# Second modulation part of the first two mixers: multiplied and added up on GpSimd between its transfers, one sum over the rows on TensorE

## Chip, cores and metric

One core of one Trainium2 chip. The metric is the device time of one execution in microseconds, median of several runs.

## What is computed

Four transformer layers on 256 tokens of width 1024, in fp32. Layers 0 and 1 have a mixer of attention, short convolution and spatial gating, and behind it a PEER layer that gathers expert rows; layers 2 and 3 have a gated linear attention and a recurrent mixer, and a mixture of 16 experts. Every layer is steered by six vectors that come from one conditioning vector, and these are what the change is about:

```python
mod = (c_act @ w_ada + b_ada)[:, None, :]            # c_act [1, 1024], w_ada [1024, 6144]
sh1, sc1, g1, sh2, sc2, g2 = jnp.split(mod, 6, axis=-1)
h = rms_norm(x, norm1_g) * (1 + sc1) + sh1
...
x = x + g1 * (merged @ w_out)
h2 = rms_norm(x, norm2_g) * (1 + sc2) + sh2
x = x + g2 * peer_ffn(h2, ...)
```

## The kernel before

**Modulation pieces.** A layer's `w_ada` is cut into three parts of 2048 columns (part 0: sh1, sc1; part 1: g1, sh2; part 2: sc2, g2), and each part into eight pieces of 128 rows x 2048 columns, 1 MB each. Piece number i is 24 x layer + 8 x part + k. The eight pieces of part 0 of layer 0 are loaded by the SP queue at the very start; all others go through a ring of six slots in `wide` (`ada_piece`, L492). GpSimd issues their loads (`ada_loads`, L599, DMA at L604) and waits before each until the slot's last piece has been read.

**Who multiplies them.** A piece contributes `c_act[128 k : 128 k + 128]` times its 128 rows. Normally TensorE does both the product and the sum over the rows: `ada_slots(n)` (L806) takes the next n pieces and issues four matmuls of 128x512 for each (L820), one per group of 32 output rows of a bank in `accs`, which gathers the eight pieces of a part. In layer 2 alone (`added`, L171) VectorE multiplies the pieces by `cact` per partition and adds them up in `ada_sums`, a seventh slot of `wide`, and `sum_added` (L826, matmuls at L832) lets TensorE sum the 128 rows once per part. Semaphores: `ada_landed` (a load is there), `ada_read` (a slot is free), `ada_added` (one step of the sum is done), `ada_summed` (TensorE has summed the rows). ScalarE copies the finished rows out (`take_rows`, L1353), TensorE turns them into columns (`mod_cols`, L838), VectorE adds the bias.

**The first two mixers.** `first_mixer` (L858) projects the input `hT` with eight slots of weights: q (two), kv, sgu (two), conv (three). A slot is 1 MB of weights in one of the two places of `ring`; the SP queue loads slot n + 2 as soon as the first matmul of slot n + 1 has ended (`load`, L547, DMA at L551; the semaphore at L739). Between slots TensorE puts one modulation piece (`ada_slots(each)`), behind the last one a batch of four, and then batches of three between the steps of the attention (`spread_over`): behind the scores, behind the mix, behind PV and behind the last transposes. That makes 8 + 16 pieces a layer: parts 1 and 2 of the layer, part 0 of the next.

The input comes from VectorE: eight multiplications of 128x256 (L1698), xT times a gain per row times `rstd`, both tensors in SBUF; ScalarE adds the shift (L1350). The first slot wants the first four of the eight blocks, the second slot the others, each matmul its own. In layer 0 the gains (L1642) are ready only when the first eight pieces are through, just ahead of these multiplications.

**GpSimd's order.** In layer 0: constants, the load of the mask data, six piece loads, the masks (`first_masks`, L680, three selects over 128x2048, 128x2048 and 128x512), the other piece loads, the load of the PEER keys. In layer 1: mask data, keys, six piece loads, masks, the other piece loads. Then the gathers of the PEER layer, which use the same slots of `wide`.

Of the kernel before, what the change touches and what calls it, by code (L numbers as in the profile page):

```python
# [18 lines left out]
P = 128  # L19
# [4 lines left out]
DEPTH = 2  # L24
# [146 lines left out]
def added(l):  # L171


    return ((l, 1), (l, 2), (l + 1, 0)) if l == DEPTH else ()


def sums_before(l):
# [10 lines left out]
def before_of(l):  # L188


    return KT + ADA_SLOTS * l


def after_of(l):

    return min(KT + ADA_SLOTS * (l + 1), LAYERS * ADA_SLOTS)
# [122 lines left out]
def program(nc, x, w, side, experts, ada, small, first_const, gla_const, keys, rows, out):  # L319


    with ExitStack() as ctx:
        def sb(name, shape, dt=F32):
            return ctx.enter_context(nc.sbuf_tensor(name, shape, dt))
# [39 lines left out]
        dots = sb("dots", [P, PICKS])  # L364
        wgt = sb("wgt", [P, 2, GROUP])
        psr = sb("psr", [P, 16])

        sel = tf[:, :, :].rearrange("p (r a) k -> p r (a k)", a=2)
        seli = ti[:, 0:2, 0:8]
# [225 lines left out]
        def _(pool):  # L595
# [3 lines left out]
            def ada_loads(first, end):  # L599


                for i in range(first, end):
                    pool.wait_ge(ada_free(i), ada_uses(i) - 1)
                    pool.dma_start(ada_piece(i), ada[i]).then_inc(  # L604
                        ada_landed[(i - ADA_FIRST) % ADA_RING], 16)

            def expert_loads(l):


                for i in range(after_of(l) - ADA_RING, after_of(l)):  # L610
                    pool.wait_ge(ada_free(i), ada_uses(i))
                pool.wait_ge(ada_summed, sums_before(l + 1))
                for i in range(OWN):
                    if i == NE:

                        tok = room(MOE["hs"], TB, D)
                        tok_hi, tok_lo = exact(MOE["tok_hi"], TB, D), exact(MOE["tok_lo"], TB, D)
                        for n in range(2 * TB):
                            b, c = divmod(n, 2)
                            u = UNIT_OF["tokens", l] + n  # L620
                            pool.wait_ge(tok_hi_ready, 2 * TB * (l - DEPTH) + n + 1)
                            wait_taken(pool, u)
                            cut = slice(c * 512, (c + 1) * 512)
                            g.tensor_tensor(tok_lo[:, b, cut], tok[:, b, cut], tok_hi[:, b, cut].bitcast(F32),
                                            ALU.subtract).then_inc(tok_lo_ready, 1)
                    at = exp_at(l, i)
                    if EXP_AT[at][0] == "arena" and i < NE:
                        pool.wait_ge(m_ready, l + 1)
                    if uses_before(l, i):
                        pool.wait_ge(exp_read[at], uses_before(l, i))  # L630
                    p, (s, half) = i // (2 * EXP_SLOTS), divmod(i % (2 * EXP_SLOTS), 2)
                    pool.dma_start(exp_slot(l, i), experts[l - DEPTH, 2 * p + half, s]).then_inc(exp_landed[at], 16)
# [62 lines left out]
            pool.dma_start(arena[:, 0:FIRST_CONST], first_const[0]).then_inc(const_landed, 16)  # L695
            ada_loads(ADA_FIRST, ADA_FIRST + ADA_RING)
            first_masks(0)
            ada_loads(ADA_FIRST + ADA_RING, after_of(0))
            pool.dma_start(keys_sb[:, :, :], keys[0]).then_inc(keys_landed, 16)
            for l in range(LAYERS):  # L700
                if l:
                    pool.wait_ge(x_ready, x_count(2 * l))
                if 0 < l < DEPTH:
                    pool.dma_start(arena[:, 0:FIRST_CONST], first_const[l]).then_inc(const_landed, 16)
                    pool.dma_start(keys_sb[:, :, :], keys[l]).then_inc(keys_landed, 16)
                elif l == DEPTH:
                    pool.dma_start(arena[:, 0:GLA_CONST], gla_const).then_inc(const_landed, 16)
                if l:
                    ada_loads(before_of(l), before_of(l) + ADA_RING)
                if 0 < l < DEPTH:  # L710
                    first_masks(l)
                if l:
                    ada_loads(before_of(l) + ADA_RING, after_of(l))
                if l < DEPTH:
                    gathers(l)
                else:
                    expert_loads(l)
# [3 lines left out]
        def _(pe):  # L721
# [40 lines left out]
            def h_counts(i, first=0, end=KT):  # L762

                return [KT * i + k + 1 for k in range(first, end)]
# [91 lines left out]
                    feature_slot(SLOT_OF["out", l] + s, UNIT_OF["out", l] + s, mT)  # L856

            def first_mixer(l):  # L858
                each = 1
                token_slots(SLOT_OF["q", l], UNIT_OF["q", l], hT, False, each, h_counts(2 * l))  # L860

                n, u = SLOT_OF["kv", l], UNIT_OF["kv", l]
                open_bank(u)
                slot_mms(n, [(bank(u)[:, b * 256:(b + 1) * 256], hT[:, k, b * P:(b + 1) * P],
                              ring[:, n % RING, k * 256:(k + 1) * 256], k == 0, k == KT - 1)
                             for b in range(TB) for k in range(KT)], {15: unit_full[u % BANKS]})
                ada_slots(each)
                token_slots(SLOT_OF["sgu", l], UNIT_OF["sgu", l], hT, adas=each)
                for s in range(3):
                    feature_slot(SLOT_OF["conv", l] + s, UNIT_OF["conv", l] + s, hT, adas=each)  # L870
                spread_over = (4, 3, 3, 3, 3)
                ada_slots(spread_over[0])
                qk = room(L1["qk"], TB, 640)
# [21 lines left out]
                        u += 1  # L895

                ada_slots(spread_over[1])
                u = UNIT_OF["conv_sum", l]
                pe.wait_ge(yc_sq, l + 1)
                open_bank(u)  # L900
# [1630 lines left out]
```

## Time and profile before

| | us |
|---|---|
| median of 3 runs | 2786.25 (2785.36 to 2791.28) |
| the profiled execution | 2792.1 |
| its span | 2790.4 |
| TensorE matmul busy | 2356.6 (84%) |
| TensorE weight load busy | 1237.1 (44%) |
| VectorE busy | 1232.2 (44%) |
| ScalarE busy | 662.0 (24%) |
| GpSimd busy | 654.5 (23%) |
| DMA moved | 934.35 MB, mean 335 GB/s |

Busy is the time in which an engine had an instruction under way. The chain is found from the last instruction backwards, at each step to what released it, so only work on the chain sets the end. PE is TensorE's matmuls, PEld its weight loads, DVE VectorE, ACT ScalarE, POOL GpSimd, SP SyncE with the queue of its loads. A matmul of fp32 counts as two in the trace, so a slot is x16 or x32 and a modulation piece x8. Spans of GpSimd are rough.

### The profile page before, as it was taken

What the parts mean: (1) busy time and instruction counts of PE and PEld (TensorE: products, weight loads), DVE (VectorE), ACT (ScalarE), POOL (GpSimd) and SP (SyncE); (2) the same over time, 40 slices, a digit from 0 to 9 for tenths busy, and PEclk for the clock granted to TensorE, in tenths of its full rate; (3) what the DMA queues carried; (4) which work ended last, traced back from release to release, by engine and by line L of the source; (5) the groups of instructions that cost most, each with busy time, mean ns of one, the idle gap of its engine ahead of it and who ended that gap; (6) DMA issues with size and microseconds to landing.
All of it is one profiled execution on the core that took longest, in us unless ns stands there. A gap on an engine that the chain in (4) does not pass through costs nothing.

```text
span 2790.4 us, 25666 instructions
## 1 busy us (share of the span) xinstructions
PE 2356.6 (84%) x9274; PEld 1237.1 (44%) x9276; DVE 1232.2 (44%) x2873; ACT 662.0 (24%) x1860; POOL 654.5 (23%) x831
## 2 busy tenths in 40 slices
PE   6999877778788989978787778887998989789988
PEld 2577433333333567433333334446443456643433
DVE  0336666776664325667767755553200022330001
ACT  1113232332233122323232323111111123111111
POOL 1103433333332102433333342101222000122200
PEclk7999998999889989999988899987999999899999
DMA  7759999999997757999999997863799235669980
GB/s 312 308 189 366 422 421 421 421 421 422 421 422 324 272 199 316 413 422 421 421 422 421 421 421 320 327 245 136 322 421 421 116 121 212 255 278 421 421 341 16
DMA packets 130126, 934.35 MB, mean 335 GB/s; under 512 B 14288, under 2 KB 16336, under 8 KB 16592
## 3 DMA queue, kind: packets, MB, share of 16 engines
q0 software_dynamic: 114768, 835.96, 72.5%
q1 hardware_dynamic: 15232, 96.75, 8.9%
q8 instruction: 74, 1.21, 0.2%
q14 instruction: 52, 0.43, 0.0%
HBM read 1070.02 MB, written 1.05 MB: 384 GB/s over the span
## 4 chain that ended last, share of the span: by engine, by line
PE 48%; DMA 30%; DVE 16%; ACT 4%; issue 2%; SPq 0%; DVEq 0%; POOL 0%; ACTq 0%; POOLq 0%
PE units L737 13%; PE units L1221 12%; DMA arena<-rows,idx 11%; PE accs L991 10%; DMA wide<-rows,idx 8%; DMA wide<-experts 5%; DMA ring<-stream 3%; DVE wide L1973 3%; DVE arena L1973 2%; PE units L752 2%; DMA arena<-experts 2%; PE units L1186 2%; PE accs L1269 2%; ACT arena L1460 1%; DMA arena<-ada 1%
## 5 line engine op out<-in xcount | busy, mean ns | idle before, releaser
L991 PE MATMUL accs<-wide,arena 128*128 128x512 f32 x1040 | 509.7, 644 | 142.4 <-ACT arena L1460 142.2
L991 PE MATMUL accs<-arena 128*128 128x512 f32 x1008 | 491.2, 643 | 93.2 <-ACT arena L1460 93.1
L991 PEld LDWEIGHTS accs<-wide,arena 128*128 128x128 f32 x1040 | 208.2, 205 | 428.7 <-issue 245.9
L1221 PE MATMUL units<-wide,arena 128*64 128x512 f32 (+1 forms) x1728 | 372.4, 602 | 26.0 <-DMA wide<-experts 21.4
L647 POOL DMA_INDIRECT wide<-rows,idx x260 | 244.9, 942 | 588.0 <-PE accs L991 408.7
L991 PEld LDWEIGHTS accs<-arena 128*128 128x128 f32 x1008 | 205.8, 208 | 375.0 <-issue 253.5
L647 POOL DMA_INDIRECT arena<-rows,idx x252 | 237.0, 940 | 369.2 <-PE accs L991 332.2
L737 PE MATMUL units<-arena,ring 128*128 128x256 f32 (+1 forms) x1344 | 299.2, 385 | 26.5 <-ACT arena L1350 14.0
L1323 ACT ACTIVATE arena<-units 128x512 f32<-128x512 f32 (+1 forms) x186 | 106.4, 574 | 839.5 <-PE units L737 299.1
L737 PEld LDWEIGHTS units<-arena,ring 128*128 128x128 f32 x1344 | 256.0, 200 | 71.1 <-issue 35.8
L1221 PE MATMUL units<-arena 128*64 128x512 f32 (+1 forms) x960 | 235.4, 594 | 17.1 <-DMA arena<-experts 10.8
L1448 ACT ACTIVATE wgt<-dots 128x4 f32<-128x4 f32 (+1 forms) x140 | 28.6, 205 | 770.3 <-DVE dots L1973 770.2
L1221 PEld LDWEIGHTS units<-wide,arena 128*64 128x64 f32 (+1 forms) x1728 | 113.3, 127 | 219.6 <-issue 216.1
L1973 DVE CUSTOM_DVE_ANT_0 arena<-arena,units 128x1024 f32<-128x1024 f32 x126 | 152.7, 1220 | 123.7 <-DMA arena<-rows,idx 123.7
L1973 DVE CUSTOM_DVE_ANT_0 wide<-wide,units 128x1024 f32<-128x1024 f32 x130 | 156.7, 1219 | 105.4 <-DMA wide<-rows,idx 105.4
L1973 DVE CUSTOM_DVE_ANT_0 arena<-arena,accs 128x1024 f32<-128x1024 f32 x126 | 151.4, 1218 | 88.8 <-DMA arena<-rows,idx 88.8
L1973 DVE CUSTOM_DVE_ANT_0 wide<-wide,accs 128x1024 f32<-128x1024 f32 x130 | 155.0, 1219 | 78.1 <-DMA wide<-rows,idx 78.1
L737 PE MATMUL units<-ring,arena 128*128 128x512 f32 (+1 forms) x352 | 151.6, 589 | 17.4 <-ACT arena L1350 8.7
L1460 ACT ACTIVATE arena<-ident,wgt 128x128 f32<-128x128 f32 x512 | 162.9, 386 | 2.5 <-PE accs L991 1.0
L2347 DVE SCALAR_TENSOR_TENSOR arena<-arena,wgt,units 128x512 f32<-128x512 f32 x22 | 16.4, 748 | 321.3 <-PE units L1221 321.3
L604 POOL DMA_DIRECT2D wide<-ada x88 | 46.5, 533 | 462.1 <-PE accs L820 272.3
L2352 DVE TENSOR_TENSOR arena_r<-units,arena_r 128x512 fp32r<-128x512 f32 x44 | 30.4, 692 | 242.6 <-ACT arena_r L1613 242.6
(317 smaller groups left out, 2154.6 us busy)
## 6 DMA issues: line engine op xcount, KB each, us to landing
wide<-experts POOLq DMA_DIRECT2D x123, 1024.0 KB, 18.3
wide<-experts SPq DMA_DIRECT2D x93, 1024.0 KB
wide<-ada POOLq DMA_DIRECT2D x88, 1024.0 KB, 10.6
arena<-experts POOLq DMA_DIRECT2D x69, 1024.0 KB, 20.3
ring<-stream SPq DMA_DIRECT2D x62, 1024.0 KB, 6.0
arena<-experts SPq DMA_DIRECT2D x51, 1024.0 KB
arena<-side SPq DMA_DIRECT2D x8, 1024.0 KB, 8.1
wide<-ada SPq DMA_DIRECT2D x7, 1024.0 KB, 16.9
```

The lines of the kernel that those rows point to most:

```text
L604: pool.dma_start(ada_piece(i), ada[i]).then_inc(ada_landed[(i - ADA_FIRST) % ADA_RING], 16)
L647: pool.indirect_dma_start(row_slot(i), None, rows[l], bass.IndirectOffsetOnAxis(ap=idx[:, n, k:k + 1], axis=0)).then_inc(row_sem(i), 16)
L737: ins = mm(o, a, b, start=start, stop=stop, skip_group_check=True)
L752: ins = mm(bank(u)[:, j * T:(j + 1) * T], side_slot(h)[:, at:at + P], hT[:, k, :], start=k == 0, stop=k == KT - 1, skip_group_check=True)
L991: ins = mm(o[:, half * 512:(half + 1) * 512], diag[:, i % (2 * GROUP), :], row_slot(PICKS * l + i)[:, D + half * 512:D + (half + 1) * 512] ...
L1186: ins = mm(bank(u)[:, j * T:(j + 1) * T], tok[:, b, k * P:(k + 1) * P], to[:, b, at:at + 2 * P], start=b + part == 0, stop=b + part == TB)
L1221: ins = mm(o[j * n:(j + 1) * n, :], act[:, j * n:(j + 1) * n], exp_slot(l, i)[:, c * 512:(c + 1) * 512], start=start, stop=stop, skip_grou ...
L1269: ins = mm(acc[d // 2][:, (d % 2) * T:(d % 2 + 1) * T], o[:, d * P:(d + 1) * P], bT, start=False, stop=p == TILES - 1 and part == 1, skip_ ...
L1323: af(o, i, func, **kw).then_inc(unit_taken[u % BANKS], 1)
L1460: ins = af(diag[:, (i + k) % (2 * GROUP), :], ident[:, :], ACT.Copy, scale=s[:, k:k + 1])
L1973: v.tensor_tensor_reduce(out=row, in0=row, in1=h, scale=1.0, scalar=0.0, op0=ALU.mult, op1=ALU.add, accum_out=dots[:, TOPK * n + k:TOPK * ...
L2352: took(tt(o_lo[:, cut], bank(u)[:, :], o_hi[:, cut].bitcast(F32), ALU.subtract), u)
```

## The change

In layers 0 and 1 part 1 goes GpSimd's way. `added` gives `((l, 1),)` for them. GpSimd does `add_piece` for the eight pieces: the first is scaled by `cact` into `ada_sums`; each other one is scaled in place and then added to `ada_sums`, with a wait on its own semaphore between the two. A memset of one column of the new tile `pad` then frees the slot, and the load of the piece six further on is issued. The remaining loads follow as before. TensorE has no piece between the slots of the projection any more (`each` is gone); it takes the 16 pieces of the batches, and behind the second batch `sum_added(l, 0)` sums the rows, once GpSimd has added all eight.

```diff
@@ def added(l):
-    return ((l, 1), (l, 2), (l + 1, 0)) if l == DEPTH else ()
+    return ((l, 1), (l, 2), (l + 1, 0)) if l == DEPTH else ((l, 1),) if l < DEPTH else ()
@@ program
+        pad = sb("pad", [P, DEPTH * KT])
@@ gpsimd
+            def add_piece(l, k):
+                i = ADA_SLOTS * l + KT + k
+                n = i - ADA_FIRST
+                pool.wait_ge(ada_landed[n % ADA_RING], 16 * (n // ADA_RING + 1))
+                w = cact[:, l // DEPTH, k:k + 1]
+                if k == 0:
+                    pool.wait_ge(c_ready, 1)
+                    if l == 0:
+                        pool.wait_ge(ada_read[ADA_RING], 1)
+                    else:
+                        pool.wait_ge(ada_summed, sums_before(l))
+                    g.tensor_scalar(ada_sums, ada_piece(i), w, None, ALU.mult).then_inc(ada_added, 1)
+                else:
+                    pool.wait_ge(ada_added, KT * sums_before(l) + k)
+                    steps(g.tensor_scalar(ada_piece(i), ada_piece(i), w, None, ALU.mult))
+                    steps.sync()
+                    g.tensor_tensor(ada_sums, ada_piece(i), ada_sums, ALU.add).then_inc(ada_added, 1)
+                pool.wait_ge(ada_added, KT * sums_before(l) + k + 1)
+                at = KT * l + k
+                g.memset(pad[:, at:at + 1], 0.0).then_inc(ada_free(i), 1)
+
+            def first_adas(l, first):
+                for k in range(KT):
+                    add_piece(l, k)
+                    ada_loads(first + ADA_RING + k, first + ADA_RING + k + 1)
+                ada_loads(first + ADA_RING + KT, after_of(l))
...
             first_masks(0)
-            ada_loads(ADA_FIRST + ADA_RING, after_of(0))
+            first_adas(0, ADA_FIRST)
...
                 if 0 < l < DEPTH:
                     first_masks(l)
-                if l:
+                if 0 < l < DEPTH:
+                    first_adas(l, before_of(l))
+                elif l:
                     ada_loads(before_of(l) + ADA_RING, after_of(l))
@@ tensor: first_mixer
-                each = 1
-                token_slots(SLOT_OF["q", l], UNIT_OF["q", l], hT, False, each, h_counts(2 * l))
+                token_slots(SLOT_OF["q", l], UNIT_OF["q", l], hT, False, fresh=h_counts(2 * l))
...
-                ada_slots(each)
-                token_slots(SLOT_OF["sgu", l], UNIT_OF["sgu", l], hT, adas=each)
+                token_slots(SLOT_OF["sgu", l], UNIT_OF["sgu", l], hT)
                 for s in range(3):
-                    feature_slot(SLOT_OF["conv", l] + s, UNIT_OF["conv", l] + s, hT, adas=each)
+                    feature_slot(SLOT_OF["conv", l] + s, UNIT_OF["conv", l] + s, hT)
...
                 ada_slots(spread_over[1])
+                sum_added(l, 0)
```

## Rows read from the trace of the kernel before

**Rows 1.** The page, chain that ended last: share of the span by engine.

```profile
PE 48%; DMA 30%; DVE 16%; ACT 4%; issue 2%; SPq 0%; DVEq 0%; POOL 0%; ACTq 0%; POOLq 0%
```

**Rows 2.** Chain that ended last, first mixer: start us, duration us, what.

```profile
48.14 9.86 PE units L737 x16
58.00 0.99 PE accs L820 x8
58.99 7.06 PE units L737 x16
...
75.25 7.06 PE units L737 x16
...
114.86 4.43 PE accs L820 x40
...
125.02 2.71 PE accs L820 x24
```

**Rows 3.** Chain that ended last, second mixer, same columns.

```profile
900.56 9.08 DMA ring<-stream
909.78 8.83 PE units L737 x32
...
959.02 4.47 PE accs L820 x40
```

**Rows 4.** Timeline, TensorE in the third layer: 48 matmuls are three slots.

```profile
1772.42 20.87 PE L737 MATMUL units<-ring,arena 128*128 128x512 f32 x48 [3.20 <-DMA ring<-stream]
1793.22 1.06 PE L832 MATMUL accs<-wide,one 128*32 128x512 f32 x8
```

**Rows 5.** GpSimd's instructions by line and shape, whole span.

```profile
L624 POOL TENSOR_TENSOR arena_r<-arena,arena_r 128x512 fp32r<-128x512 f32 x8 | 9.9, 1256 | 98.4 <-ACT arena L1323 98.4
L684 POOL TENSOR_SCALAR_AFFINE_SELECT arena<-arena 128x2048 f32<-128x2048 f32 x2 | 3.9, 1954 | 1.7 <-DMA arena<-first_const 1.7
L692 POOL TENSOR_SCALAR_AFFINE_SELECT arena<-arena 128x512 f32<-128x512 f32 x2 | 1.3, 668 | 0.1
```

**Rows 6.** Timeline, GpSimd and VectorE side by side, second and third layer.

```profile
886.19 1.94 POOL L684 TENSOR_SCALAR_AFFINE_SELECT arena<-arena 128x2048 f32<-128x2048 f32 x1 [1.69 <-DMA arena<-first_const]
888.28 1.94 POOL L687 TENSOR_SCALAR_AFFINE_SELECT arena<-arena 128x2048 f32<-128x2048 f32 x1
886.24 2.18 DVE L1698 SCALAR_TENSOR_TENSOR arena<-xT,gains_of,rstd 128x256 f32<-128x256 f32 x1
886.24 7.01 DVE L1698 SCALAR_TENSOR_TENSOR arena<-xT,gains_of,rstd 128x256 f32<-128x256 f32 x8
...
1943.09 1.27 POOL L624 TENSOR_TENSOR arena_r<-arena,arena_r 128x512 fp32r<-128x512 f32 x1 [47.42 <-ACT arena L1323]
1943.25 1.12 DVE L2187 TENSOR_TENSOR tf<-tf 128x8 f32<-128x8 f32 x1
```

**Rows 7.** Two issues near 76 us, their landings, one landing near 1773 us.

```profile
75.58 0.53 POOL L604 DMA_DIRECT2D wide<-ada  x1 [7.66 <-PE accs L820]
76.34 0.33 SPq L551 DMA_DIRECT2D ring<-stream  x1
ring<-stream SPq DMA_DIRECT2D x1, 1024.0 KB, 6.9
...
ring<-stream SPq DMA_DIRECT2D x1, 1024.0 KB, 4.7
```

**Rows 8.** Timeline, first layer: GpSimd's last mask, then VectorE ahead of the mixer.

```profile
37.10 0.63 POOL L692 TENSOR_SCALAR_AFFINE_SELECT arena<-arena 128x512 f32<-128x512 f32 x1
...
44.98 0.17 DVE L1642 SCALAR_TENSOR_TENSOR gains_of<-mods_of,cols 128x8 f32<-128x8 f32 x1
46.96 3.26 DVE L1698 SCALAR_TENSOR_TENSOR arena<-xT,gains_of,rstd 128x256 f32<-128x256 f32 x8
```

**Rows 9.** DMA issues at 15.5 and 881.3 us: KB, us to landing.

```profile
wide<-ada POOLq DMA_DIRECT2D x1, 1024.0 KB, 9.3
...
wide<-ada POOLq DMA_DIRECT2D x1, 1024.0 KB, 9.6
```

## The prediction

> **What bounds the kernel now.** I read the page's chain first, to see whose work is worth removing. TensorE holds 48% of it and GpSimd 0% [rows 1], so on average the change takes work from the right engine and gives it to an idle one. That average says nothing of the two stretches that are touched, so I followed the chain through them. In the first mixer it stays on TensorE: slots of the projection (58.99 us, 7.06) alternate with one modulation piece each (58.00 us, 0.99) until 114.86 us, where the batch of pieces behind the last slot begins [rows 2]. In the second mixer it is the same, except that the third slot waits for its weights from 900.56 to 909.64 us; the batch begins at 959.02 us [rows 3]. What a removed piece is worth is read where slots follow each other bare: three slots take 20.87 us, 6.96 each [rows 4]. From 58.99 to 114.86 us there are seven slots and six pieces: 55.87 less 7 x 6.96 is 7.15, so 1.19 us a piece.
>
> **What is removed.** Eight pieces in each of two mixers: seven behind slots, and of the five pieces in the batch (4.43 us) one, 0.89 us. If nothing else moved, the first mixer's slots would end at 58.0 + 48.7 = 106.7 in place of 114.9 us. In the second mixer two pieces stand ahead of the third slot and only one counts: its weights are issued one piece (1.0 us) earlier and, as I let them take the same 9.08 us, it starts at 908.8 in place of 909.8; it stays at 8.83 us, and five bare ones end at 952.4 in place of 959.0. The 0.89 of the batch comes on top, twice.
>
> **What is added on TensorE.** One sum over the 128 rows per mixer, the four matmuls that the third layer shows at 1793.22 us: the next slot starts 1.0 us on [rows 4]. It stands between batches that are on the chain, so it counts in full. With the batch's 0.89 this is +0.1 a mixer.
>
> **What is added on GpSimd.** Per piece one scaling of 128x2048 in place, one addition of 128x2048, a memset and the issue of a load. A scaling has one input like the masks of that size: 1.95 us [rows 5]. An addition has two inputs; the only row is 128x512 at 1.256. Four times that is 5.02; with the fixed part taken off that the masks of 2048 and 512 elements give (0.24 us), it is 4.3. I take 4.3, since the fixed part is paid once, and keep 5.0 as the end of the range. The hand-over behind a wait is 0.15 us (888.28 less 886.19 and 1.94 [rows 6]); five of these are 0.75, the load's issue 0.53 [rows 7]. Together 1.95 + 4.3 + 0.53 + 0.8 = 7.6 us a piece, 8.3 at the upper end. *The Trainium skill (GPSIMD Engine Reference, Performance versus the Vector engine) gives 4.497 us for an addition of 2048 elements; by it a piece is 7.8 us and the sum below 2.6 us higher. No run here has that shape yet.* In the first layer GpSimd is free of masks at 37.73 us [rows 8], its first piece landed at 24.8 [rows 9], and its eight loads are issued from 40.3 us on (37.73 + 1.95 and four hand-overs), every 7.6 us, to 93.5. In the second the last mask, of 0.67 us, ends at 891.0 and the first piece lands at 890.9 (881.3 + 9.6): loads from 893.5 to 946.7 us. TensorE reaches its sum behind the batch of 125.02 us, so the sum itself waits for nobody. The eight loads are those of the next pieces, now queued behind additions; the last of them land about 5 us after 93.5 and 946.7, before TensorE's second batch wants them (125.02 [rows 2], and as much behind the first batch in the second layer). The keys' load stays behind the last piece and moves with TensorE. So the new engine's time is hidden. Two side effects are not.
>
> **First side effect: GpSimd holds VectorE up.** In the second layer the eight multiplications that make the mixer's input run beside the masks and take 7.01 us where the first layer takes 3.26 [rows 6, 8]. The first needs 2.18 us: it ends just after the mask of 886.19 + 1.94. Each mask lets one multiplication through and then holds the next. An addition does the same: a VectorE operation of 128x8 takes 1.12 us, to the end of the 1.27 us one on GpSimd. In the first layer these multiplications stand at 46.96 us on the chain and GpSimd is idle there until now [rows 8]. With additions at 43.1 to 47.4, 50.9 to 55.2 and 58.9 to 63.2 us and scalings between, the gains (44.98) slip to 47.4, the first multiplication ends at 50.9, the second at 55.6, two more in the gap behind the addition, the fifth at 58.8, the rest after 63.2. TensorE starts at 51.5 and waits for the second block until 56.2. A bare slot has eight pairs of 0.87 us, the first slot took 9.86, so the four pairs behind an idle stretch took 1.6 each; again so, it ends at 56.2 + 3 x 1.6 + 4 x 0.87 = 64.5 in place of 58.0: +6.5 us. At least it is nothing. At most no multiplication passes between two pieces either: then the eight spread over four pieces, the second slot ends near 84 us, the mixer is 10.6 us longer in place of 0.3 (below) and the whole sum +5.5. I take the middle way because a load's issue computes nothing. In the second layer only the last ones meet the first piece, and they belong to the second slot: 0. *The Trainium skill (SBUF — State Buffer, Who interferes with whom) has a rule that speaks against this change: a VectorE instruction with two SBUF inputs and a GpSimd instruction that reads SBUF exclude each other for a whole instruction, while a GpSimd instruction that only writes, as a memset, holds nobody. For the masks the trace agrees (2.18 us beside 1.94); by the rule multiplications pass between pieces and the sum is -4.8 us, by the widest reading of the rows it is +5.5.*
>
> **Second side effect: loads meet weights.** The slot's weights are issued when the slot before has begun, 1.1 us in (76.34 against 75.25 [rows 2, 7]). Alone they land after 4.7 us, with a piece issued 0.76 us earlier after 6.9: weights issued in its wake land 7.7 us after its issue [rows 7]. Before, this fitted the 8.06 us from slot to slot exactly. Bare slots want them after 6.96. GpSimd's loads come every 7.6 us whatever TensorE does, and a slot that has caught up with them cannot start before such an issue + 7.7. First layer: slots from 64.5 would end at 113.2; the issues at 78.3, 85.9 and 93.5 push the starts to 86.0, 93.6 and 101.2, the end to 115.1, against 114.9: +0.2, with the 0.1 it is +0.3. Second layer: starts 908.8, 917.6, then the issues of 916.3 to 939.1 give 924.6, 931.6, 939.3, 946.8, end 953.8 against 959.0: -5.2, with the 0.1 it is -5.1.
>
> **Sum**: -4.8 us, 0.17% of the time. The profiled execution took 2792.1 us, 5.9 above the median of 2786.25; on its basis this is 2787.3, on the median's 2781.5, which I forecast. A measurement of this kernel can tell about 0.2% (5.6 us) from no change. With the addition at 5.0 us the sum is +4.3.
>
> **Rivals.**
> (a) Neither side effect bites. For it: the longest hold in the rows is 2.2 us, none is of an addition this long, and loads issued just behind the weights would not delay them. Against it: 7.01 beside 3.26. Then first mixer -8.2 + 0.1, second -6.6 + 0.1: -14.6, 2771.7 us.
> (b) Only one bites. Only the hold: first -1.7 + 0.1, second -6.5, together -8.1, 2778.2. Only the loads: the first slots start at 58.0 but the last issue still rules, end 108.2, so -6.6 - 5.1 = -11.7, 2774.6.
> (c) Slower: GpSimd's pace rules. Each 0.1 us on a piece moves the last issue by 0.7 and 0.6 us. At 8.3 the sum is +4.3, at 8.4 it passes +5.6, at 8.5 it is +6.9, 2793.2 us; past 8.8 the loads fall behind the weights, which then land alone, and the loss goes, until from 10.5 us on the late loads of the sixth to eighth piece hold TensorE's second batch. For it: the addition has no row of its size, and VectorE's operations hold GpSimd in turn. Against it: 5.0 us for the addition is already four whole short ones.
> (d) That the pieces are not taken off TensorE is excluded by the edit: its list skips what is in the table of additions.
>
> **Numbers.** Forecast as worked out 0.55 (its own range, by an addition of 4.0 to 5.0 us, 2777.5 to 2791; about a quarter of it lies below -5.6 us), (a) 0.12, (b) 0.16, (c) 0.17. Faster by over 0.2%: 0.14 + 0.12 + 0.16 = 0.42; slower: 0.17 and 0.01 of the forecast, 0.18; within 0.40. The range goes from between (a) and (b), 2773, to just past (c), 2794.
>
> **What would show it.** GpSimd: 14 additions of 4.3 us, loads about 7.6 us apart, done by about 95 and 948 us. VectorE's eight multiplications in the first layer spread over more than 12 us, the first slot ending near 65. Slots at 6.96 where no load was issued shortly before their weights, 7.6 where one was, the batch beginning near 115.1 and 953.8. The forecast is wrong if the eight multiplications stay under 5 us, if slots beside loads run at 6.96, or if the loads are over 8.4 us apart.

## The result: slower by 0.8%, and the profile after

| | before | after |
|---|---|---|
| median of 4 runs each, us | 2785.82 (2785.36 to 2791.28) | 2812.36 (2806.21 to 2817.46) |
| ratio after/before, 95% interval | | 1.0077 (1.0049 to 1.0104) |
| profiled execution, us | 2792.1 | 2806.21 |
| its span, us | 2790.4 | 2804.5 |

The ratio is +21.5 us (13.7 to 29.0), while the two medians of the table lie 26.5 us apart and the two profiled executions 14.1 us. The forecast was 2781.5 us, that is -4.8, with a range of 2773 to 2794: both the side and the range were wrong.

The page of the kernel after, the chain that ended last by engine, against [rows 1]: GpSimd had 0% of it and has 3%, some 80 us.

```profile
PE 44%; DMA 30%; DVE 17%; ACT 4%; POOL 3%; issue 2%; SPq 0%; DVEq 0%; POOLq 0%; ACTq 0%
```

GpSimd's instructions by line and shape in the kernel after, against [rows 5] (behind the x its count, then busy us, then mean ns of one). L625 is the scaling in place, L622 the first piece's scaling (into the sums, not in place), L627 the addition:

```profile
L625 POOL TENSOR_SCALAR wide<-wide,cact 128x2048 f32<-128x2048 f32 x14 | 76.5, 5464 | 0.6
L627 POOL TENSOR_TENSOR wide<-wide 128x2048 f32<-128x2048 f32 x14 | 64.0, 4569 | 1.2
L622 POOL TENSOR_SCALAR wide<-wide,cact 128x2048 f32<-128x2048 f32 x2 | 11.0, 5485 | 0.1
```

The addition is where it was expected, 4.57 us against 4.3. The scaling takes 5.46 us against 1.95: it has one input and is slower than the addition, which has two. A piece is thus 11.1 us and not 7.6.

**The first mixer.** Timeline of the kernel after, GpSimd and VectorE side by side, against [rows 8] (start us, duration us):

```profile
44.92 5.46 POOL L625 TENSOR_SCALAR wide<-wide,cact 128x2048 f32<-128x2048 f32 x1
45.65 3.03 DVE L1676 SCALAR_TENSOR_TENSOR gains_of<-mods_of,cols 128x8 f32<-128x8 f32 x1
48.71 1.75 DVE L1727 RECIPROCAL rstd<-rstd 128x256 f32<-128x256 f32 x1
50.46 4.49 POOL L627 TENSOR_TENSOR wide<-wide 128x2048 f32<-128x2048 f32 x1
50.50 11.15 DVE L1732 SCALAR_TENSOR_TENSOR arena<-xT,gains_of,rstd 128x256 f32<-128x256 f32 x8
```

The gains took 0.17 us before and 3.03 now, the eight multiplications 3.26 and now 11.15. The reciprocal of 48.71, with one input, runs its usual 1.75 us while the scaling of 44.92 is still at work; in e8 below one of 47.33 takes the same 1.75 us beside an addition of 47.34 to 51.84. Chain that ended last, kernel after, first mixer, against [rows 2]:

```profile
55.92 23.98 PE units L772 x66
79.92 6.21 DMA ring<-stream
86.17 20.96 PE units L772 x80
...
108.30 4.02 DVE arena L1796
...
117.08 5.29 DVE arena L1816 x2
...
125.84 7.66 PE units L925 x30
133.50 3.72 PE accs L855 x24
137.22 0.86 PE accs L867 x8
```

TensorE starts its slots at 55.92 in place of 48.14. The bare slots make that good: the batch of pieces begins at 115.48 us, against 114.86 before. What they do not make good comes behind them. From 108 to 124 us the chain is on VectorE: its operations on queries and keys (L1796 took 1.49 us before) and those of the convolution (the two of L1816, 0.62 us together before, though each multiplies one tensor by a column and has no second tensor) are held too, because GpSimd is still at its pieces; its last addition ends at 122.2 us. The product behind them (L925) starts at 125.84 in place of 120.98, and takes 7.66 us in place of 4.04, and the granted clock says why. Two windows show this product alone, first 126 to 133 us after, then 121 to 125 us before (window, its length, busy us and count of TensorE, its weight loads, VectorE, ScalarE and GpSimd, granted clock, DMA share, GB/s):

```profile
126.00:133.00 7.00, 7.00 (x32) 6.12 (x32) 5.04 (x10) 2.24 (x10) 0.00 (x0) 0.50 1.02 426
```

```profile
121.00:125.00 4.00, 4.00 (x36) 3.47 (x40) 3.22 (x6) 0.00 (x0) 0.00 (x0) 1.00 1.02 430
```

TensorE idled for 5.5 us ahead of it after, for 0.45 before, and does the product at 0.50 (1.2 GHz) in place of 1.00 (2.4 GHz). The next product (L937) starts at 138.08 in place of 127.73: +10.35, of which 4.86 is the later start, 3.62 the slower product, 1.01 the batch (3.72 in place of [rows 2]'s 2.71), 0.86 the sum.

**The second mixer.** Chain that ended last, kernel after, second mixer, against [rows 3]. The load issued at 985.76 is that behind GpSimd's last piece; the one after it follows at once, lands at 993.41 and ends the chain of waits:

```profile
901.09 5.53 POOL wide L622
...
907.70 5.47 POOL wide L625
913.24 4.51 POOL wide L627
...
974.61 0.60 POOL wide L605
...
985.76 0.60 POOL wide L605
...
986.36 7.05 DMA wide<-ada
...
995.38 1.07 PE accs L867 x8
```

Here the chain is GpSimd's own, piece after piece, for 85 us. TensorE's timeline shows the other end of it: its matmuls of the next pieces each wait for a load (the bracket is the idle time before, and what ended it), about 11.2 us apart as GpSimd issues them.

```profile
960.56 2.78 PE L855 MATMUL accs<-wide,cact 128*32 128x512 f32 x24
...
968.60 1.93 PE L855 MATMUL accs<-wide,cact 128*32 128x512 f32 x8 [5.26 <-DMA wide<-ada]
...
979.80 1.93 PE L855 MATMUL accs<-wide,cact 128*32 128x512 f32 x8 [2.91 <-DMA wide<-ada]
...
990.98 1.93 PE L855 MATMUL accs<-wide,cact 128*32 128x512 f32 x8 [9.24 <-DMA wide<-ada]
```

With the last one (0.54 us of idle time at 993.45) these are 17.9 us of waiting. In the kernel before TensorE has no wait for a piece in this stretch: its batches of 958.95, 969.12 and 974.63 us start without idle time for one.

**A ledger of the two mixers.** Runs of one kernel lie up to 0.7% apart, so I compare traces by marks inside them. VectorE computes a reciprocal at the start of each norm. The first mixer is the time from the span's start to the second of them, the second mixer the time from the third to the fourth:

```profile
193.62 1.75 DVE L1693 RECIPROCAL rstd<-rstd 128x256 f32<-128x256 f32 x1 [3.08 <-ACT rstd L1323]
...
884.45 1.75 DVE L1693 RECIPROCAL rstd<-rstd 128x256 f32<-128x256 f32 x1 [4.26 <-ACT rstd L1323]
...
1043.44 1.75 DVE L1693 RECIPROCAL rstd<-rstd 128x256 f32<-128x256 f32 x1 [3.08 <-ACT rstd L1323]
```

That is the kernel before; the same marks after, where the line is L1727:

```profile
204.01 1.75 DVE L1727 RECIPROCAL rstd<-rstd 128x256 f32<-128x256 f32 x1 [3.08 <-ACT rstd L1357]
...
894.57 1.75 DVE L1727 RECIPROCAL rstd<-rstd 128x256 f32<-128x256 f32 x1 [4.26 <-ACT rstd L1357]
...
1062.07 1.75 DVE L1727 RECIPROCAL rstd<-rstd 128x256 f32<-128x256 f32 x1 [3.08 <-ACT rstd L1357]
```

One group has to be taken out. The same 48 matmuls (L934 before, L968 after) stand once in each mixer, at either level of TensorE's clock: chains of before (first two lines) and of after.

```profile
142.63 5.32 PE units L934 x48
...
987.19 10.15 PE units L934 x48
```

```profile
152.88 5.32 PE units L968 x48
...
1011.42 6.01 PE units L968 x48
```

In before's 987 to 997 us the granted clock is 0.50, in 142 to 148 us it is 0.96. TensorE has idled for 4.75 us, with 3.7 us of work behind that, ahead of the group at 987.19 as ahead of the one at 1011.42; what else decides the level stays open. Over the kernels below this group takes 5.3 to 6.1 us or 10.1, in either mixer, so I subtract it. Left are, for before, 188.30 and 148.84 us; for after 198.69 and 161.49: **+10.4 and +12.7, together +23.0 us**, near the 21.5 of the ratio. The profiled executions themselves lie only 14.1 us apart: after's groups of 48 are 4.1 us shorter than before's, its stretch behind the second mixer 4.5 us, and what lies between the mixers 0.3 us. Without that subtraction the second mixer would show +8.5, and 4 us of its loss would be hidden by the clock.

### The profile page after: what moved, and what is told of

It reads as the page before. It is cut to its first block, busy times and chain, and to the rows that moved or that the text cites. A ratio compares the mean times of both kernels' runs of the same rounds, so it can differ in the third digit from the quotient of the medians.

```text
span 2804.5 us, 25506 instructions
## 1 busy us (share of the span) xinstructions
PE 2329.4 (83%) x9164; PEld 1227.8 (44%) x9164; DVE 1285.0 (46%) x2873; ACT 662.5 (24%) x1860; POOL 808.8 (29%) x877
## 3 DMA queue, kind: packets, MB, share of 16 engines
q1 hardware_dynamic: 15232, 96.75, 9.0%
## 4 chain that ended last, share of the span: by engine, by line
PE 44%; DMA 30%; DVE 17%; ACT 4%; POOL 3%; issue 2%; SPq 0%; DVEq 0%; POOLq 0%; ACTq 0%
PE units L1255 11%; DMA arena<-rows,idx 11%; PE accs L1025 10%; PE units L772 10%; DMA wide<-rows,idx 8%; DMA wide<-experts 5%; DMA ring<-stream 4%; DVE wide L2007 3%; DVE arena L2007 2%; PE units L787 2%; DMA arena<-experts 2%; PE units L1220 2%; PE accs L1303 2%; POOL wide L625 1%; ACT arena L1494 1%
## 5 line engine op out<-in xcount | busy, mean ns | idle before, releaser
L1025 PE MATMUL accs<-arena 128*128 128x512 f32 x1008 | 481.2, 632 | 98.6 <-ACT arena L1494 98.6
L1255 PE MATMUL units<-arena 128*64 128x512 f32 (+1 forms) x960 | 235.5, 594 | 17.4 <-DMA arena<-experts 11.2
L665 POOL DMA_DIRECT2D wide<-experts x123 | 64.8, 529 | 279.3 <-PE units L1255 233.7
```

The source lines that it names most:

```text
L1025: ins = mm(o[:, half * 512:(half + 1) * 512], diag[:, i % (2 * GROUP), :], row_slot(PICKS * l + i)[:, D + half * 512:D + (half + 1) * 512] ...
L1255: ins = mm(o[j * n:(j + 1) * n, :], act[:, j * n:(j + 1) * n], exp_slot(l, i)[:, c * 512:(c + 1) * 512], start=start, stop=stop, skip_grou ...
```

## The experiments

The theory after the result: the scaling's length sets GpSimd's pace (late loads in the second mixer), and GpSimd's reads hold VectorE (first mixer). The rivals: the hold alone does it; the pace alone does it; or the loads that meet the weights do. All kernels start from the changed one. The ledger of all of them (us against before, the 48 matmuls taken out; the issues are the median of the first mixer's eight; ratios with intervals where timed in rounds, a single time for e3, e6 and e8):

| kernel | load issues apart, us | first mixer | second mixer | time, ratio to before |
|---|---|---|---|---|
| after | 11.1 | +10.4 | +12.7 | 1.0077 (1.0049 to 1.0104) |
| e1 | 5.6 | +6.6 | -4.1 | 0.9973 (0.9959 to 0.9987) |
| e2 | 10.3 | 0.0 | +11.3 | 0.9994 (0.9976 to 1.0011) |
| e3 | 11.1 | +7.0 | +14.4 | 2809.92 us |
| e4 | 2.5 | -2.1 | -3.9 | 0.9978 (0.9959 to 0.9996) |
| e5 | 7.9 | -4.4 | -7.9 | 0.9962 (0.9946 to 0.9978) |
| e6 | 11.1 | +19.9 | +14.6 | 2826.84 us |
| e7 | 5.6 | -7.8 | -2.3 | 0.9934 (0.9908 to 0.9960) |
| e8 | 9.3 | +4.8 | +10.6 | 2803.91 us |

Each ledger is of one profiled execution. After and e3 have instructions of nearly the same length and differ by 3.4 and 1.7 us, so a difference of 3 us between two kernels says little; those that the verdicts rest on are 6 us and more, but for e4 to e5, where first and second mixer point the same way, and e8's +4.8 in the first mixer. The stretch between the two mixers, which no edit touches, is up to 5.2 us longer than before (e2).

**Whole times of e1, e2 and e7 are not to be read against before.** They leave out part of the computation, and one DMA queue then carries less. The page's row of that queue (packets, MB, share) in e1 and e2 (before has 96.75 MB there):

```profile
q1 hardware_dynamic: 14368, 90.46, 8.5%
```

```profile
q1 hardware_dynamic: 13504, 84.17, 7.9%
```

e1 and e7 move 6.3 MB less, e2 12.6 MB less; at the 421 GB/s of the transfer-bound slices 6.3 MB are 15 us, by an estimate. Which loads those are was not looked into; that other values lead to other loads of experts' weights is argued, not shown. What lies behind the second mixer is 15.2, 13.3 and 7.5 us shorter in e1, e2 and e7 than before, and within 4.6 us of it in the other kernels. So the bytes do not give the size (e1 and e7 leave out the same 6.3 MB), but these ledgers count and the totals do not. This was no part of the expectations: e2's 2788.97 us lies below the 2795 to 2805 expected, and e1's 2780.23 below the 2798 of its hold theory, without speaking against either theory. e3 has other values too, but moves the 96.75 MB of before.

### e1: no scaling in place (each piece added as it is, seven of eight pieces of a mixer unscaled)

```diff
-                    steps(g.tensor_scalar(ada_piece(i), ada_piece(i), w, None, ALU.mult))
-                    steps.sync()
```

> Leaves out GpSimd's scaling of the seven later pieces (they enter the sum unscaled), so GpSimd adds only. Pace theory (the scaling, 5.46 us, makes a piece 11.1 us, and the last loads come too late for TensorE's second batch): a piece takes 5.7 us, the last of the eight loads is issued near 84 and 940 us instead of 122.7 and 985.8, TensorE's second batch waits for no load, and the time falls to 2780 to 2790 us. Hold theory (VectorE's two-input operations wait for each GpSimd instruction, and that is most of the loss): the additions of 4.5 us still hold it, the eight multiplications of the first layer still take 8 us or more, and the time stays above 2798 us.

Measured: a piece takes 5.6 us, the last of the eight loads is issued at 84.13 and 942.53 us, and the late loads are gone from the second mixer, -4.1. The first stays at +6.6, and the hold grew: with additions back to back the eight multiplications take 21 us in place of after's 11.15 (timeline of e1).

```profile
52.19 21.05 DVE L1730 SCALAR_TENSOR_TENSOR arena<-xT,gains_of,rstd 128x256 f32<-128x256 f32 x8
```

Pace and hold are two mechanisms: the pace is the second mixer's loss, and in the first the hold alone, with pieces half as long, still costs 6.6 us against before and 14.4 against e7 below, which differs by its absence.

### e2: GpSimd only writes (every piece's scaling and addition replaced by memsets of 128x2048, so the sums are zero)

The cut shows the seven later pieces; the first piece's scaling becomes three memsets.

```diff
-                    steps(g.tensor_scalar(ada_piece(i), ada_piece(i), w, None, ALU.mult))
-                    steps.sync()
-                    g.tensor_tensor(ada_sums, ada_piece(i), ada_sums, ALU.add).then_inc(ada_added, 1)
+                    for _ in range(4):
+                        steps(g.memset(ada_sums, 0.0))
+                        steps.sync()
+                    g.memset(ada_sums, 0.0).then_inc(ada_added, 1)
```

> GpSimd does no arithmetic on the pieces: in place of scaling and addition it writes zeros over the sum, five memsets of 128x2048 a piece (estimate 2.0 us each with the wait, 10 a piece, three for the first piece), so its pace stays near that of the changed kernel while it reads nothing. Hold theory: the eight multiplications take 3.3 us in the first layer instead of 11.2, the operations on q and k take their time of before, the first mixer gets back 8 to 11 us. Pace theory: in the second mixer the last load is still issued near 985 and TensorE's second batch still waits for it, so at least 8 us of that mixer's loss stay. Both true: 2795 to 2805 us. If memsets hold VectorE as well, nothing changes in either mixer.

Measured: GpSimd is as busy (five memsets of 1.81 us, issues 10.3 us apart), and its memsets hold neither the eight multiplications nor L1796's counterpart (1.49 us, as before). Timeline of e2, the gains aside:

```profile
47.86 3.26 DVE L1736 SCALAR_TENSOR_TENSOR arena<-xT,gains_of,rstd 128x256 f32<-128x256 f32 x8
```

They do hold the multiplications of one tensor by a column in the convolution (L1816 in after, here L1820): 2.32 us in place of 0.62, to the end of a memset, and 3.71 in the second mixer. They are not on e2's chain.

```profile
108.13 2.32 DVE L1820 TENSOR_SCALAR arena<-arena,cols 128x256 f32<-128x256 f32 x2
```

The first mixer is at 0.0, the second at +11.3 with the late load on its chain (e2's chain, the second mixer; the first has 7.12 us of the same at 116.89):

```profile
979.75 7.07 DMA wide<-ada
```

So in the second mixer the pace alone gives nearly the whole loss. In the first, the late load eats all that the bare slots gain, since e7 without it is at -7.8; and of the step from 0.0 to +10.4 not all is the hold's, since the last load is issued at 116.37 us in e2 and at 122.71 in after. By that estimate up to 6.3 us are the slower pace's, and the hold's own part is between 4 and 10 us.

### e3: the same scaling with the constant 0.5 in place of the factor from a column

```diff
-                    g.tensor_scalar(ada_sums, ada_piece(i), w, None, ALU.mult).then_inc(ada_added, 1)
+                    g.tensor_scalar(ada_sums, ada_piece(i), 0.5, None, ALU.mult).then_inc(ada_added, 1)
...
-                    steps(g.tensor_scalar(ada_piece(i), ada_piece(i), w, None, ALU.mult))
+                    steps(g.tensor_scalar(ada_piece(i), ada_piece(i), 0.5, None, ALU.mult))
```

> The scaling takes the constant 0.5 in place of a factor per partition (so the sums are scaled by 0.5 and not by the condition). If the factor per partition is what makes 128x2048 take 5.46 us, the scaling falls to near the 1.95 us of the masks, a piece takes 7.6 us, and the time is that of my forecast, 2778 to 2791 us. If it is the instruction itself, it stays at 5.4 to 5.5 us and the time at 2806 to 2817.

Measured: 5.40 us, as with the column, and 2809.92 us, as expected for that case. It is not the factor's fetch. In after, the first piece's scaling (L622, into another tile) at 5.49 shows that it is not the writing in place either.

### e8: the scaling as a multiplication of two tensors, the factor broadcast

```diff
-                    steps(g.tensor_scalar(ada_piece(i), ada_piece(i), w, None, ALU.mult))
+                    steps(g.tensor_tensor(ada_piece(i), ada_piece(i), w.broadcast_to([P, SLOT]), ALU.mult))
```

> GpSimd's scaling as a product of two tensors, the factor broadcast over the row. Theory that a GpSimd instruction of this size costs by what it reads: 4.5 us as the addition, a piece 10.2 in place of 11.1 us, the last load of mixer two issued 7 us earlier than 985.8 and that mixer 6 to 7 us shorter than in the changed kernel. If the product form is as slow as the scaling, 5.4 to 5.5 us and nothing changes.

GpSimd's scaling in e8 (its additions take 4.83 us):

```profile
L625 POOL TENSOR_TENSOR wide<-wide,cact 128x2048 f32<-128x2048 f32 x14 | 50.6, 3614 | 0.3
```

The same product costs 3.61 us in this form against 5.46 as a scaling. So it is the instruction's form that is slow, and neither expectation (4.5 us, or 5.4 to 5.5) was met. A piece is 9.3 us, and yet the mixers lose 15.4 us (the second was expected 6 to 7 us below after's and is 2.1 below): the eight multiplications now take 22 us in the first layer. The second mixer shows where that pace leads when it no longer makes loads late: the chain there has no wait for a piece's load, but held VectorE operations again, L1796 and L1816 (chain of e8):

```profile
950.46 5.06 DVE arena L1796
...
961.11 8.21 DVE arena L1816 x2
```

### e6: the change, but GpSimd starts in the first layer only when VectorE's eight multiplications are done

```diff
                         pool.wait_ge(ada_read[ADA_RING], 1)
+                        pool.wait_ge(hx_ready, KT)
```

> The changed kernel with one more wait: in the first layer GpSimd starts on the pieces only when VectorE's eight multiplications are done, 12 us later. Hold theory: the multiplications take 3.3 us and the first slot ends near 58. Pace theory: all eight loads are then 12 us later, the last issued near 135 us in place of 122.7, and TensorE's second batch, at 133.5 us in the changed kernel, waits for it until after 142, so mixer one ends later than in the changed kernel though nothing held its start: 162 to 170 us against 158.6.

Measured: the multiplications are back at 3.26 us and the first mixer is 9.5 us worse than after. The eighth load is issued at 135.71 in place of 122.71, 13.0 us later; the ninth follows it at once and is on e6's chain, with the last piece of TensorE's second batch behind it:

```profile
135.71 0.60 POOL wide L605
136.31 7.08 DMA wide<-ada
143.44 1.94 PE accs L856 x8
```

In the changed kernel that piece, issued 13.0 us earlier, would land near 130.4, and TensorE reads it as the third of the batch of 133.50, from about 136.3 (0.9 us before the sum of 137.22): some 5.9 us of slack, so 7.1 us are the late load. The other 1.9 us up to the next product (147.08 against 138.08) are the clock, as TensorE had idled for 8.54 and 0.60 us: at 0.50 the piece takes 1.94 us and the sum 1.71, in after at 1.00 they take 0.9 and 0.86. So in the first mixer the pace stands only some 6 us behind the hold, and whoever takes the hold at its start away by starting later meets the late loads. From its modulation to the next norm this mixer takes 172.6 us (about 168 with the group of 48 at the length that it had in after), and 162 to 170 were expected.

### e7: e1 and e6 together (unscaled additions, late start)

```diff
                         pool.wait_ge(ada_read[ADA_RING], 1)
+                        pool.wait_ge(hx_ready, KT)
...
-                    steps(g.tensor_scalar(ada_piece(i), ada_piece(i), w, None, ALU.mult))
-                    steps.sync()
```

> As the run without scaling, but in the first layer GpSimd starts its additions only when VectorE's eight multiplications are done. Hold theory: they take 3.3 us again instead of over 20, TensorE starts on the first slot near 48.5 us instead of 53, and since eight additions of 5.7 us from 51 us on are done by 97 no piece comes late: mixer one, 153.9 us from its modulation to the next norm in the run without scaling, falls to 143 to 147 us (before: 148.9). Rival (the loads meet the weights, the hold costs little): it stays above 150.

Measured: the first mixer is at -7.8 us, and 145.5 us from its modulation to the next norm, where 143 to 147 were expected. The pace of 5.6 us has GpSimd finished by 96 us, before VectorE's operations on queries, keys and the convolution, and its start is behind the multiplications. The hold is gone and no piece's load is late, and the figure is what removing eight pieces was said to be worth there (-8.1). Chain of e7, first mixer: bare slots but for two whose weights are on the chain. The DMA lines are the weights' whole time from issue to landing, most of which runs beside the slot ahead; TensorE stands still for 0.63 and 0.68 us of it:

```profile
48.51 9.37 PE units L771 x18
57.89 6.47 DMA ring<-stream
64.50 14.88 PE units L771 x50
79.39 6.52 DMA ring<-stream
```

The second mixer was left as in e1: its multiplications take 10.49 us beside masks and additions, and three slots' weights take 9.0, 7.1 and 8.4 us to land, for which TensorE stands still for 3.11, 1.21 and 2.58 us.

### e4 and e5: VectorE multiplies and adds in one instruction, behind its eight multiplications; GpSimd only loads

The edit moves the pieces to VectorE, as the third layer has them: there scaling and addition are one instruction of 2.35 us, in place of 10 us on GpSimd. e5 also lets GpSimd issue each load only when a slot's weights have landed, so that loads and weights alternate. Its core:

```diff
+                n0 = SLOT_OF["q", l]
                 for k in range(KT):
-                    add_piece(l, k)
+                    if 0 <= k - 2 * (l == 0) < 6:
+                        s = n0 + 2 + k - 2 * (l == 0)
+                        pool.wait_ge(slot_landed[s % RING], 16 * (s // RING + 1))
                     ada_loads(first + ADA_RING + k, first + ADA_RING + k + 1)
...
                 s3 = room(L1["sq3"], 1024)
+                for k in range(KT):
+                    add_piece(l, 0, k)
```

> The same pieces are multiplied and added on VectorE, one instruction each as in the third layer, directly behind the eight multiplications; GpSimd only issues the loads. VectorE is idle there for over 20 us, eight times 2.5 us fit, nothing on GpSimd reads SBUF. Pace and hold theory both: no hold, no late load; both mixers end earlier than before by up to 7 us each, 2771 to 2780 us. If instead the loads, now as fast as every 2.5 us, delay the weights by more than a slot's spare time, the third slot waits 3 to 6 us in each mixer and the time is 2780 to 2786.

> As the run with VectorE's additions, but the loads no longer go out as fast as pieces are added: from the third on in the first layer, and from the first on in the second, each waits until the weights of one more slot have landed, and so goes between two slots' weights. Meeting theory (in that run the burst of loads made TensorE wait 9.7 and 9.2 us for weights in mixer one and 9.5, 9.0, 9.1 in mixer two, each a wait of 2 to 3 us beyond a bare slot): slots at 6.96 to 7.1 us throughout, mixer one 6 to 8 us shorter than before (it was 2.2), mixer two 8 to 10, together 2772 to 2778 us with before at 2789.9. If the waits had another cause, mixer one stays 2 us shorter and the time at that run's 2786.

Measured: neither has a hold or a late load, and both are shorter than before in both mixers, so loads that meet weights do not make the change's loss by themselves. In e4 the eight loads come in a burst, 2.5 us apart, and the weights behind them take 9 to 9.7 us to land. e4's chain, the first mixer:

```profile
58.77 9.74 DMA ring<-stream
```

TensorE works on the slot ahead for most of that time; it stands still for 3.90 us here, for 2.89 before the next slot and for 3.65, 0.59 and 3.13 in the second mixer, 14.2 us in all. e4's 2786.05 us is thus the second of its two expectations, at its upper end.

VectorE's line of the pieces in e5 (14 of the 35 are those of the two mixers), and then e5's chain, first mixer, where TensorE stands still for 0.85 and 0.80 us at the ends of the two loads:

```profile
L1713 DVE SCALAR_TENSOR_TENSOR wide<-wide,cact 128x2048 f32<-128x2048 f32 x35 | 82.3, 2352 | 13.2 <-DMA wide<-ada 13.2
```

```profile
72.64 6.79 DMA ring<-stream
...
80.63 6.64 DMA ring<-stream
```

e5 spreads them, weights take 6.3 to 7.4 us to land, TensorE's waits are 1.1 us at most (8.4 us in all), and it gains 6.2 us of ledger on e4; the intervals of the two ratios overlap, so the ledger alone shows that gain. It leaves nothing of the computation out and is faster than before: 0.9962 (0.9946 to 0.9978), 2779.12 us beside 2790.41 on the same chip; the changed kernel is at 1.0077. Its ledger, -12.3 us, and its ratio, -10.6 us, agree. The expectation was missed all the same: slots were to come at 6.96 to 7.1 us, the first mixer to be 6 to 8 us shorter than before and the time 2772 to 2778. The slots come about 8 us apart (in the first mixer from 79 us on), with a wait of 0.4 to 1.1 us ahead of each, and the first mixer is 4.4 us shorter (the second 7.9, where 8 to 10 were expected). So spacing takes away the long waits, not the meeting itself; where a load must be issued to cost nothing was not tried.

## Why the prediction was wrong

**The step that failed** is the first of "What is added on GpSimd": "A scaling has one input like the masks of that size: 1.95 us". It took 5.46 us. A row of another instruction of the same shape was taken as a price, with no bound on the other side; the addition got two bounds, the scaling none. That is +3.5 us a piece, nearly the whole way from 7.6 to 11.1. With the addition's 4.3 to 5.0 us as the scaling's upper bound a piece would have come to 10 to 11.4 us, past the 10.5 from which (c) had the late loads hold TensorE.

**A second step was too cheap**, and the right price of the scaling would not have saved it: the hold in the first mixer, which with the loads was to leave +0.3 us there. e1 and e8, whose pieces are shorter than after's (5.6 and 9.3 us), still lose 6.6 and 4.8 us in that mixer. What a pace of 7.6 us with a scaling of 1.95 would have held was not run.

**The addition** was right: 4.57 us, between the 4.3 taken and the 5.0 kept. The Trainium skill (GPSIMD Engine Reference, Performance versus the Vector engine) had 4.497; e1 shows 4.53. By that page's figure the forecast sum would still have been -2.2 us: the error was in the other term.

**Rival (c), "GpSimd's pace rules"**, is what happened, but not at its price. It had the threshold and the place: from 10.5 us on, the late loads of the sixth to eighth piece hold TensorE's second batch. At 11.1 they do, in the second mixer. I gave that no time, and (c)'s chance of 0.17 was priced at 8.5 us a piece, since with the addition at 5.0 us a piece reached 8.3 only. e2 waits for a late load at a pace of 10.3 us in both mixers, so the threshold of 10.5 was slightly high; e8 at 9.3 does not, though e8's TensorE also asks later, as its VectorE is held.

**First side effect, the hold:** the mechanism was right, its reach too small. The multiplications took 11.15 us (over 12 was said), and the gains 3.03. TensorE started 7.8 us late; I had the first slot 6.5 us late. As forecast, one multiplication ends just behind the addition (at 55.24) and others pass in the gap behind it; not as forecast, the scaling holds the rest too. Additions back to back (e1) give 21 us for the eight: the widest reading let no multiplication pass between two pieces either. e2 confirms the rule of the Trainium skill (SBUF — State Buffer, Who interferes with whom) that I weighed for VectorE's operations with two inputs: GpSimd writing alone does not hold the eight multiplications (3.26 us), reading it holds them (11.15). My "holds nobody" was too wide: the rule says it of two-input operations, and beside memsets the one-input multiplications by a column took 2.32 us for 0.62. Nor does a hold last the whole instruction, as I had it: a scaling lets go earlier (below). Missed was that the same holds wherever GpSimd still runs: VectorE's operations on queries, keys and the convolution from 108 to 124 us, and through them TensorE's clock. At a pace of 7.6 us the additions would have been over by 94. So this part hangs on the scaling; in e7, where GpSimd is done by 96 us, the same operations take 1.49 and 0.62 us, as before.

**Second side effect, loads meet weights:** real, and what is left once the others are gone: TensorE's 14.2 us of waits for weights in e4 and 8.4 in e5 are it. In the changed kernel itself it is small: in the first mixer TensorE stands still for 0.28 and 1.28 us, in the second for 1.33 and 0.29. The batch began at 115.48 us against 115.1 forecast, in the second mixer at 960.56 against 953.8 forecast, with the mixer itself starting 10.1 us later than before: 66.0 us behind its reciprocal, where the forecast had 69.3 (953.8 less 884.45). The second mixer's slots did better than forecast, the first's as forecast; the loss is all behind them.

**What is removed, and the sum on TensorE:** right, as far as the first mixer shows. Rival (a) had -8.1 us there with neither side effect; e7 measured -7.8. The second mixer's -6.5 no run shows bare: e5 comes to -7.9. The sum took 0.86 and 1.07 us where 1.0 was said.

**"TensorE reaches its sum behind the batch of 125.02 us, so the sum itself waits for nobody"** holds for the sum, whose last addition ends at 985.3 us, and not for the batches ahead of it: in the second mixer the sum is at 995.38, 34.8 us behind the first batch's start at 960.56, because the pieces' loads are late.

What stays open: why GpSimd needs 5.46 us for a scaling that it does in 3.61 us as a product of two tensors. In the trace of after VectorE gets through 3.8 us after such a scaling has begun (44.92 to 48.68), and again 3.7 us after that of 112.07 (L1800, 0.69 us long, ends at 116.43). So there the last 1.7 us or so of it hold nobody. No run tells what that part is.

## What to carry to other kernels

Price an instruction by a row of that very operation, and where there is none, bound it above by the dearest estimate for its shape, and above that leave room: here a one-input scaling cost more than a two-input addition. Before work moves to an engine that is idle on average, multiply out its pace per item against the consumer's, and ask where its last item falls: everything queued behind it (here eight loads) moves with it, and VectorE's operations that meet it can wait for it (11.15 us for 3.26 here). One fused VectorE instruction of 2.35 us with spaced loads did what 10 us of GpSimd could not.

## What the runs showed that was not expected

- GpSimd, 128x2048 in 32-bit floats: scaling 5.46 us with a factor from a column, 5.40 with a constant; product with a broadcast factor 3.61; addition 4.53 to 4.83; memset 1.81; mask 1.95.
- Additions and products of two tensors on GpSimd, one behind the other, hold VectorE longer than additions with a scaling between: 21.05 us (e1) and 22.07 (e8) for eight multiplications, 11.15 in after, 3.26 with nobody or with memsets. Two multiplications of one tensor by a column on VectorE are held by both: 5.29 us beside additions (after), 2.32 beside memsets (e2), 0.62 alone. A reciprocal of one tensor is not held (1.75).
- A kernel whose data are changed for an experiment can move other amounts elsewhere (6.3 and 12.6 MB less here, beside 7.5 to 15.2 us less in a stretch that the edit does not touch, where the effect under study is 21.5 us). Look at the bytes per queue before a total is believed.
- TensorE waiting 5.5 us for a held VectorE had its next product at 0.50 of the clock in place of 1.00, 3.6 us: an indirect cost of an instruction on GpSimd. The clock also gave one group of 48 matmuls 5.3 or 10.15 us between kernels that are alike there, nearly as much as the second mixer's forecast gain of 5.1.
